# Attention units from four blocks of keys down to one, with the sample work at the same steps

## The reference

```python
o = (gates[:, :, 0, :, None] * o_c.astype(jnp.float32)
     + gates[:, :, 1, :, None] * o_s.astype(jnp.float32)
     + gates[:, :, 2, :, None] * o_w.astype(jnp.float32))
```

## Time and profile before

| | |
|---|---|
| runs (median of 3) | 3304.2 us (3303.33 to 3307.55) |
| profiled execution: time | 3302.38 us |
| its span | 3300.7 us |
| TensorE busy (its share of the span) | 3006.9 us (91%) |
| VectorE busy | 1828.3 us (55%) |
| ScalarE busy | 1285.2 us (39%) |
| GpSimd busy | 76.6 us (2%) |
| mean granted TensorE clock | 0.961 of full speed |

### The profile page before, as it was taken

How to read it: one execution, slowest core, us unless ns; L and a number is a source line. 1 busy time by engine, 2 the same in 40 slices (tenths; PEclk the granted TensorE clock), 3 DMA queues, 4 the chain that set the end, 5 groups by cost and what they waited for, 6 DMA issues and landing times. The chain is left out here.

```text
span 3300.7 us, 73320 instructions
## 1 busy us (share of the span) xinstructions
PE 3006.9 (91%) x30540; PEld 2812.0 (85%) x30540; DVE 1828.3 (55%) x3293; ACT 1285.2 (39%) x2278; POOL 76.6 (2%) x140
## 2 busy tenths in 40 slices
PE   5988988999899898789999888999979889889997
PEld 5975588999899787589999888999969755889997
DVE  3346646636467665656365665646533466466364
ACT  2236534323255332233233683423322365343232
POOL 0002100000000000000000000000000021000000
PEclk9989999999999898899999998999989899999999
DMA  6635304222222001223322322422266353042222
GB/s 192 205 110 174 110 26 171 86 94 81 74 87 84 25 2 59 103 95 135 103 87 64 105 66 83 144 90 98 70 155 205 110 173 110 27 171 85 94 81 78
DMA packets 156079, 339.44 MB, mean 103 GB/s; under 512 B 58884, under 2 KB 93316, under 8 KB 143380
## 3 DMA queue, kind: packets, MB, share of 16 engines
q1 hardware_dynamic: 146836, 296.04, 28.2%
q0 software_dynamic: 7424, 37.76, 3.2%
q10 hardware_dynamic: 1536, 1.60, 0.2%
HBM read 318.40 MB, written 32.12 MB: 106 GB/s over the span
## 5 line engine op out<-in xcount | busy, mean ns | idle before, releaser
L471 PE MATMUL ffn_ps<-ffn_x_hi_sb,ffn_w_hi_sb 128*128 128x260 f32 x2816 | 571.9, 285 | 49.4 <-DVE ffn_w_lo_sb L592 46.2
L471 PE MATMUL ffn_ps<-ffn_x_hi_sb,ffn_w_lo_sb 128*128 128x260 f32 x2816 | 571.1, 285 | 0.0
L471 PE MATMUL ffn_ps<-ffn_x_lo_sb,ffn_w_hi_sb 128*128 128x260 f32 x2816 | 570.5, 285 | 0.0
L471 PEld LDWEIGHTS ffn_ps<-ffn_x_hi_sb,ffn_w_hi_sb 128*128 128x128 f32 x2816 | 438.4, 190 | 51.8 <-DVE ffn_w_lo_sb L592 47.9
L471 PEld LDWEIGHTS ffn_ps<-ffn_x_hi_sb,ffn_w_lo_sb 128*128 128x128 f32 x2816 | 438.2, 190 | 0.0
L471 PEld LDWEIGHTS ffn_ps<-ffn_x_lo_sb,ffn_w_hi_sb 128*128 128x128 f32 x2816 | 437.2, 190 | 0.0
L526 ACT ACTIVATE ffn_w_hi_sb<-ffn_raw_sb 128x2048 fp32r<-128x2048 f32 (+2 forms) x148 | 249.3, 1684 | 338.5 <-PE ffn_ps L471 338.5
L549 ACT ACTIVATE ffn_pre_sb<-ffn_ps 128x520 f32<-128x520 f32 x176 | 106.5, 605 | 601.7 <-PE ffn_ps L471 313.8
L607 DVE SCALAR_TENSOR_TENSOR ffn_conv_sb<-ffn_pre_sb,ffn_conv_w_sb,ffn_conv_sb 128x512 f32<-128x512 f32 x176 | 132.4, 752 | 341.3 <-ACT ffn_conv_sb L551 341.3
L586 DVE TENSOR_TENSOR ffn_w_lo_sb<-ffn_raw_sb,ffn_w_hi_sb 128x2048 fp32r<-128x2048 f32 (+2 forms) x148 | 296.0, 2000 | 44.8 <-ACT ffn_w_hi_sb L526 44.8
L471 PE MATMUL ffn_ps<-ffn_inner_hi_sb,ffn_w_hi_sb 128*128 128x260 f32 x1408 | 284.9, 284 | 6.5 <-DVE ffn_inner_lo_sb L625 3.4
(11 more groups left out here) (496 smaller groups left out, 5695.9 us busy)
## 6 DMA issues: line engine op xcount, KB each, us to landing
ffn_raw_sb<-ffn_w_in SPq DMA_DIRECT2D x84, 1024.0 KB, 4.8
ffn_raw_sb<-ffn_w_out SPq DMA_DIRECT2D x32, 768.0 KB, 4.2
nsa_ring_sb<-sel_pages SPq DMA_DIRECT2D x160, 128.0 KB, 2.5
ffn_raw_sb<-ffn_w_out SPq DMA_DIRECT2D x32, 640.0 KB, 3.9
nsab_page_slot_sb<-cmp_pages SPq DMA_DIRECT2D x64, 256.0 KB
all_xn_t_sb<-cmp_pages SPq DMA_DIRECT2D x64, 256.0 KB
gdnp_w_raw_sb<-gdn_w_in SPq DMA_DIRECT2D x30, 512.0 KB, 3.8
nsab_w_raw_sb<-nsa_w_in SPq DMA_DIRECT2D x28, 512.0 KB, 5.9
```

What stands on the lines that cost most here:

```text
L471: mm = pe.matmul(psf[:, bank + h, 0:H], wp[:, w[0], w[1]:w[1] + P], xp[:, h * H:(h + 1) * H], start=start and k == 0, stop=stop and k == 2)
```

## The change

The list of units is built with the blocks of queries in falling order: first the eight units with four blocks of keys, then those with three, two and one. Nothing else is edited: the steps at which the sample work runs, the semaphores, the buffers and the loads stay. Since the sample work keeps its step numbers, it now meets other units: keys of s = 4, 8 and 14 fall among four-block units, those of 20, 26 and 31 among three-block units, softmax, turns and the first four values (33 to 47) among two-block units, the last two values and the join (50 to 59) among one-block units.

```diff
-    units = [(i, t) for i in range(NCH) for t in range(KT)]
+    units = [(i, t) for i in reversed(range(NCH)) for t in range(KT)]
```

## The result

The changed kernel takes 3312.5 us (median of 17 runs, 3303.8 to 3322.2) against 3305.0 us of the kernel before beside it (17 runs, 3303.0 to 3309.2). The forecast was 3303.0 us and no change; the range ended at 3311. The new kernel also scatters more widely: 18 us against 6 here, and 12 over 35 runs of the kernel before beside the first experiments.

A forecast was written before the change was run, and what follows sets the result against it. A PE-DVE ring was taken as the bound. Per layer 0.5 - 7.1 - 1.8 + 4.5 - 0.5 + 2.6 + 1.2 = -0.6 us, -1.2 in all: 3301.2 us profiled, 3303.0 as median, range 3297 to 3311.

The forecast's parts named there:

- an early return of the clock and one more short fall, +4.5: Stage start, s=0 to s=6: longer by 4.5 us per layer, between +3.9 at full clock and +6.7 at half clock.
- short fall of the clock, 1.2 us: Join: PE idling behind DVE lets the clock fall briefly, adding 1.2 us per layer.
- Rings: s=6 to s=62: 28 rings through PE and DVE, their sum nearly unchanged by the order, +0.5 us per layer.
- sample items: Sample keys and values at their fixed steps meet units of other lengths: -0.5 us per layer.
- loads: Window values, used at s=53, are tightest with 4.4 us spare: cost 0, +0 to +2 us kept for contention.
- End: Scores of s=62 to first projection: 6.26 us with one-block units instead of 13.39, -7.1 us per layer.
- The -1.8 us behind it: Behind the projection's start: 24 fewer value matmuls and 6 fewer transposes between projections, -1.8 us per layer.
- DVE's excess: s=55 to 59: join and weights exceed DVE's slack by 1.0, 2.25 and 0.95 us, 4.2 against 1.5 before: +2.6 per layer.
- 2.4 in one piece: Join: PE idles about 2.4 us at once, its turn waiting for the scaling queued behind DVE's work.
- Rival A: From s=57 on: clock stays down behind the join, 13.7 us at half clock, +10.1 us, 3314.3 us; chance 0.13.
- upper end of 23.5: Stage start, s=0 to s=6: slowest case, +6.7 us, with PE at half clock until 246.2.
- +3.9: Stage start: lower end, 3.9 us longer per layer at full clock, s=6 at 252.8.

The follow-up runs named there:

- the first experiments: Earliest follow-up kernels, with extra unused matmuls or another unit order, each compared with the kernel before on the same chip; the text does not list which.
- both filled: Changed kernel plus extra unused matmuls in PE's waits at the join and at the stage's start: 3300.3 us, 0.9991 of the kernel before.
- early placement: Changed kernel with sample work moved to even steps 4 to 34 and the join to 35: 3300.0 us, 0.9987; with extra matmuls at the start 3298.5 us.
- the start filled: Changed kernel plus four extra unused matmuls ahead of the stage and four behind the scores of step 1, none at the join: 3304.2 us, 1.0002.
- the old order with a filled start: Kernel before, its unit order kept, plus the same extra unused matmuls at the start of the stage: 3303.0 us, 0.9996.
- the same placement: Sample work on even steps 4 to 34, join at 35, extra matmuls at the start: 3298.5 us in the falling order, 3340.9 us in the rising one.

## Why the prediction was wrong

Two terms of the sum failed, both of the clock. The start, "an early return of the clock and one more short fall, +4.5", came out at +10.5 us in the first stage and +4.7 in the second, and filling it takes away 7 us of the 7.6. The "short fall of the clock, 1.2 us" at the join came out at 4.3 and 3.3 us in the trace. The other terms hold.

**Rings, sample items, loads: right.** Plain rings are the same in either order, s=6 to s=62 came out at 181.2 against 181.0 (180.2 with both filled, against 179.8 without the fall at the join), and no load is late.

**End: right.** The forecast had 6.26 us from s=62 to the projection; at full clock it is 6.49 and 6.50 (both filled, early placement), at half clock 7.87. The -1.8 us behind it shows too. From its first matmul to the end of its last, the projection takes 50.5 us in all eight stages that end with four-block units, and 48.5 or 48.6 in all six that end with one-block units and begin it at full clock: -1.9. Where a fall reaches into it, it takes 49.3 to 50.7. What varies without a pattern is the way from there to the feed-forward part, 13.7 to 14.6 us.

**Join: DVE's excess right, the clock under-sized.** From s=54 to the projection the forecast, without its fall of the clock, is 4 x 3.58 + 4.2 + 6.26 = 24.8 us; in the second stage of the kernel with both filled it took 25.1. The three dearer rings came one ring later than named, at s=56, 58 and 60: longer there, with both filled, by 1.06, 2.15 and 1.06 us, against 1.0, 2.25 and 0.95. The pause was named at the right place:

```profile
427.63 0.49 PE L2546 MATMUL nsat_ps<-nsa_kv_sb,nsa_q_rotated_sb 64*128 64x128 f32 x4
...
429.45 0.33 PE L2563 MATMUL nsat_ps<-all_consts_sb,nsat_prob_sb 128*128 128x128 f32 x1 [1.22 <-DVE nsat_prob_sb L2792]
...
435.44 1.07 PE L2563 MATMUL nsat_ps<-all_consts_sb,nsat_prob_sb 128*128 128x128 f32 x2 [0.83 <-DVE nsat_prob_sb L2792]
...
450.60 0.80 PE L201 MATMUL nsat_ps<-nsa_y_hi_sb,nsat_w_hi_sb 128*128 128x260 f32 x2
```

PE waits 1.22 us for DVE (not 2.4 in one piece), where six instructions of the join, the last four of them below, stand ahead of the next maximum; later DVE waits for the sample's placing:

```profile
426.76 1.51 DVE L2845 SCALAR_TENSOR_TENSOR all_xn_t_sb<-nsat_ps,nsat_s_factor_sb,all_xn_t_sb 128x128 f32<-128x128 f32 x4
428.18 0.41 DVE L2775 TENSOR_REDUCE nsat_nmax_sb<-nsat_ps 128x2 f32<-128x256 f32 x1
...
433.21 0.80 DVE L2853 TENSOR_TENSOR nsat_y_lo_sb<-nsat_ps,nsa_y_hi_sb 64x32 fp32r<-64x32 f32 x4 [1.56 <-ACT nsa_y_hi_sb L2735]
```

From 430.5 on the clock is down, and it stays down until the projections have run for 3.8 us. The step that failed here is "a short fall of the clock, 1.2 us (half of a few us ...)". It lasted 17 to 24 us: from s=54 (423.15) to the projection (450.60) it is 27.5 us, 2.4 more than with both filled, and the projection's first 3.8 us at half speed add up to 1.9; in the second stage it is 2.4 and 0.9. Rival A's mechanism was the right one; its price of half the duration was too high, since at half clock PE only fills the time it would have waited for DVE. The ring at s=60 took 4.81 us at half clock and 4.64 at full clock with its filling. Between the kernels with the start filled and with both filled it is 1.0002 - 0.9991 = 0.11%, 3.6 us or 1.8 a layer; the two intervals make that uncertain by 0.14%, so the medians do not show this cost, and with both filled one stage still had a fall at its projection. That A's 3314.3 us lies near the 3312.5 measured is luck: A puts the whole loss at the join, and most of it was at the start.

**Start: the term that failed most.** "An early return of the clock and one more short fall, +4.5" rested on PE's wait getting shorter and its first scores filling the time. At full clock but for one short fall the start took 20.99 us, +4.2, close to that, and the changed kernel's second stage came to 21.44. In its first stage the clock did not come back early. The rest of the pause does not go away: after the scores of s=0 and s=1, PE still stands for the maximum and the exponentials. Timeline of PE in the changed kernel, first stage:

```profile
238.05 0.46 PE L2552 MATMUL nsat_ps<-all_causal_sb,all_ident_sb 64*128 64x128 bf16 x4
240.22 2.08 PE L2546 MATMUL nsat_ps<-nsa_kv_sb,nsa_q_rotated_sb 64*128 64x512 f32 x4 [1.71 <-ACT nsat_prob_sb L2694]
...
245.16 1.97 PE L2563 MATMUL nsat_ps<-all_consts_sb,nsat_prob_sb 128*128 128x128 f32 x8 [0.62 <-DVE nsat_prob_sb L2792]
246.92 3.42 PE L2589 MATMUL nsat_ps<-nsa_kv_sb,nsat_q_s_sb 128*128 128x8 f32 x16
...
254.39 2.90 PE L2607 MATMUL nsat_ps<-nsa_ring_sb,nsat_q_s_sb 128*32 128x512 f32 x16
```

Everything to 256.4 runs at half speed (scores 2.08 instead of 1.13), and four blocks make that dear: 27.35 us, beyond the upper end of 23.5, which took the clock back at 246.2 as before. Filling the start is worth 1.0023 - 1.0002 = 0.21%, 7 us (uncertain by 4), against 1.2 in the forecast (twice 4.5 - 3.9). Up to 4 of them the fill could also give the old order.

The Trainium skill, "TensorE: Matmul & The Clock Gate", section "Part 1: The HAM clock gate", has half rate as the default that activity releases. The traces agree: with the wait inside the stage filled the clock stays at 1.00 from 235.6 on, and with the same matmuls ahead of it PE is busy 1.21 of 3.40 us and the next stretch is at half clock. The +3.9 that the prediction read from this rule came only with the start filled (+4.2); unfilled, the starts were at +10.5 and +4.7. The section calls the price of warming up less than 1% of a typical span; filling the start took away 0.2% here, which agrees, and is nearly all of the change.

**What the sum was worth without the clock.** With the start at +3.9 and no fall at the join the prediction's terms give -2.4 us a layer, -4.8 in all; both filled measured -3.0 [-6.3, +0.7], which agrees and cannot be told from nothing. Part by part, the second stage of the kernel with both filled has 20.99, 180.2, 6.49 and 63.1 us against 20.7, 179.8, 6.26 and 63.1. So the terms without the clock were costed right against this kernel before, whose own start loses time to the clock; against the first stage of the old order with a filled start, 3.6 us shorter at the start, the same terms give +1.2 us, and the traces +2.0. As differences of ratios, +7.0 for the start, +3.6 for the join and -3.0 for the rest make the 7.6 measured; only the first is clear of the noise.

**What stays open.** Why the clock returns in one stage within 3.4 us and in the other after 24, with the same instructions, is not shown. That the scatter of 18 us comes from it is likely, not shown: two profiled executions of filled kernels with both starts at 20.99 us took 3302.9 and 3305.3 us and the changed kernel's with 27.35 took 3315.2, but no second execution of one kernel was traced.

## What to carry to other kernels

Where units of different length run through a ring of engines as here, their order moves only the ends and what is hung on fixed steps; before gaining at an end, look at what TensorE waits for there, since each pause can bring half clock for longer than the pause itself. Price a fall of the clock with at least the longest stretch that the trace shows (13.7 us before, and 23.9 came), not with a short one, and test it with a few matmuls that nothing uses, put inside the waits. Fill both kernels before saying what an order is worth: the one before may be losing time to the clock as well. Work hung on steps should go where the units are long and their transfers have time: the same placement, with the start filled, gained 6 us in the falling order and cost 38 in the rising one.

## What the runs showed of the hardware

A stretch at 1.2 GHz can far outlast the wait ahead of it: with PE busy 22.71 of 23.90 us behind the join the granted clock stayed at 0.50, and it rose when the projection had run for 3.8 us (1.8 in the second stage). One wait of 1.22 us, besides the 0.26 and 0.42 us of plain rings, stood ahead of that fall. Half clock costs less than half its length where PE waits for another engine anyway: a ring behind the join took 4.81 us at 0.50 and 4.64 at 1.00, where PE also had three extra matmuls. Four matmuls, 2.2 us of work, changed the median by 10 us when moved from ahead of the first scores to behind those of step 1 (3317.1 and 3307.0 us on one chip).
